# Gate, up, value and state-space gate projections as unit pairs with 512 moving weight columns

## What is computed

```python
def swiglu(u, w_gate, w_up, w_down):
    return (jax.nn.silu(u @ w_gate) * (u @ w_up)) @ w_down
...
    v = (mem_n @ wv).reshape(b, m, XATTN_HEADS, XATTN_HEAD_DIM)
...
    y = y.reshape(b, S, SSM_D_INNER) * jax.nn.silu(z.astype(jnp.float32))
```

## Time and profile before

| what | us |
|---|---|
| median of 3 runs | 2004.78 (2002.03 to 2006.02) |
| the profiled execution | 2001.61 |
| its span, first to last instruction | 1999.7 |
| TensorE busy | 1965.3 (98%) |
| GpSimd busy | 1567.7 (78%) |
| ScalarE busy | 1041.5 (52%) |
| VectorE busy | 720.5 (36%) |

### The profile page before, as it was taken

One profiled execution on the slowest core, in us unless ns is written; L12 is line 12 of the kernel. 1 busy time (PEld: TensorE's weight loads), 2 busy tenths in 40 slices (PEclk: granted clock), 3 DMA queues, 4 the chain that ended last, 5 costly groups with the idle time before them and its releaser, 6 DMA issues.

```text
span 1999.7 us, 34347 instructions
## 1 busy us (share of the span) xinstructions
PE 1965.3 (98%) x14430; PEld 1861.1 (93%) x14430; DVE 720.5 (36%) x1300; ACT 1041.5 (52%) x1342; POOL 1567.7 (78%) x1226
## 2 busy tenths in 40 slices
PE   7999999999999999999999999999999999999998
PEld 7999999988999999999999889999989999999997
DVE  2540866421200231037663320004687843022001
ACT  6434684456534554357644764346655556445333
POOL 7889786666888789878686759887686787789995
PEclk9999999999999999999999999999999999999999
DMA  8455543143555465554323445555433344445552
GB/s 319 170 199 189 186 144 114 64 169 134 203 190 189 173 231 182 187 181 178 127 78 135 169 150 188 190 190 196 147 127 120 127 156 148 158 179 195 181 185 104
DMA packets 48538, 332.60 MB, mean 166 GB/s; under 512 B 5376, under 2 KB 6272, under 8 KB 10112
## 3 DMA queue, kind: packets, MB, share of 16 engines
q1 hardware_dynamic: 43920, 314.60, 43.9%
q10 hardware_dynamic: 4464, 15.80, 2.3%
HBM read 329.33 MB, written 1.05 MB: 165 GB/s over the span
## 4 chain that ended last, share of the span: by engine, by line
PE 85%; DVE 6%; ACT 4%; POOL 1%; DVEq 1%; issue 1%; ACTq 1%; DMA 1%; SPq 0%
PE bank L1673 23%; PE bank L1674 23%; PE bank L1675 23%; ACT arena L371 2%; PE bank L1786 1%; POOL wlo L350 1%; PE bank L2029 1%; PE bank L2045 1%; ACT whi L371 1%; PE bank L1766 1%; PE bank L1768 1%; DVE x L1005 1%; DVE arena L978 1%; DVE bank L993 1%; PE bank L2152 1%
## 5 line engine op out<-in xcount | busy, mean ns | idle before, releaser
L350 POOL TENSOR_TENSOR wlo<-raw,whi 128x512 fp32r<-128x512 f32 x1188 | 1526.4, 1323 | 375.3 <-ACT whi L371 375.3
L1673 PE MATMUL bank<-uT_hi,whi 128*128 128x256 f32 x2560 | 731.5, 286 | 0.0
L1674 PE MATMUL bank<-uT_lo,whi 128*128 128x256 f32 x2560 | 725.2, 283 | 0.0
L1675 PE MATMUL bank<-uT_hi,wlo 128*128 128x256 f32 x2560 | 725.2, 283 | 0.0
L371 ACT ACTIVATE whi<-raw 128x2048 fp32r<-128x2048 f32 x297 | 566.8, 1910 | 170.0 <-PE bank L1675 152.3
L1673 PEld LDWEIGHTS bank<-uT_hi,whi 128*128 128x128 f32 x2560 | 491.6, 192 | 3.5 <-issue 1.4
L1674 PEld LDWEIGHTS bank<-uT_lo,whi 128*128 128x128 f32 x2560 | 491.6, 192 | 3.3 <-issue 1.4
L1675 PEld LDWEIGHTS bank<-uT_hi,wlo 128*128 128x128 f32 x2560 | 491.5, 192 | 0.0
L371 ACT ACTIVATE arena<-bank 128x512 f32<-128x512 f32 (+3 forms) x285 | 153.8, 554 | 337.6 <-PE bank L1675 264.9
L1053 DVE TENSOR_TENSOR bank<-arena,bank 128x512 f32<-128x512 f32 x50 | 34.8, 696 | 606.3 <-PE bank L1675 606.3
L1673 PE MATMUL bank<-whi,hT_hi 128*128 128x512 f32 x440 | 172.0, 391 | 0.0
(11 more groups left out here) (269 smaller groups left out, 2596.7 us busy)
## 6 DMA issues: line engine op xcount, KB each, us to landing
raw<-in_w SPq DMA_DIRECT2D x297, 1024.0 KB, 4.8
rows<-in_rows ACTq DMA_DIRECT2D x23, 512.0 KB, 4.9
arena<-in_mem ACTq DMA_DIRECT2D x2, 1024.0 KB, 7.2
x<-in_x SPq DMA_DIRECT2D x2, 512.0 KB, 6.4
out<-x SPq DMA_DIRECT2D x2, 512.0 KB, 2.7
arena<-in_amask ACTq DMA_DIRECT2D x1, 768.0 KB, 7.8
cst<-in_cst SPq DMA_DIRECT2D x1, 452.0 KB, 12.6
arena<-in_lvl SPq DMA_DIRECT2D x1, 384.0 KB, 13.9
```

Source lines behind the costliest of these rows:

```text
L350: r = pool.tensor_tensor(wlo[n % LAND][:, k], raw[n % LAND][:, k], whi[n % RING][:, k].bitcast(F32), ALU.subtract)
L1673: pe.matmul(o, l[0], r[0], start=start, stop=False)
L1674: pe.matmul(o, l[0], r[1], start=False, stop=False)
L1675: return pe.matmul(o, l[1], r[0], start=False, stop=stop)
```

## The change

- A new packing, `pair`, replaces two `cols` units by two units that each hold 512 columns over half of the depth (four 128-row blocks of 512 columns).
- `pair_unit` and `pair_half` work on them: for each half, token tile 0 into one bank and tile 1 into the other, 12 matmuls of 512 columns each. A new semaphore `tok_half` tells that tile 0 is complete, 12 matmuls before `unit_done` of the second unit.
- In a feed-forward block a bank now holds 256 gate columns and 256 up columns of one token tile. ACT and DVE work on each tile apart (256 columns an instruction), and the product goes to an SBUF buffer, `h_tok`. TensorE transposes it back in every chunk (`h_transposes`, two 128 x 128 transposes for each tile), after the down unit of the chunk before; in the last chunk one tile ahead of each half of the work of tile 0 in `last_rows`.
- `first_pair` runs on such pairs: for tile 0 high and low of half 0, high of half 1, the transposes of tile 1, low of half 1.
- Memory values (two pairs a layer), the first two retention value units, the first two units of the attention queries and the gates z use pairs as well. Their ACT readers wait for `tok_half` or for the second unit.

```diff
-                    act.wait_ge(sems["unit_done"], g + 1)
-                    fn(sg[q], bank[4 + 2 * q if c else 0][:, :], AF.Silu).then_inc(sems["silu_gate"], 1)
-                    split()
+                    if c:
+                        split()
                     if memory and c in (3, 4):
                         memory_hi(c - 3, (4, 6)[c - 3])
-                    if c:
-                        act.wait_ge(sems["ff_product"], p.count("ff_product"))
+                    for t in range(NT):
+                        if t == 0:
+                            act.wait_ge(sems["tok_half"], p.count("tok_half"))
+                        else:
+                            act.wait_ge(sems["unit_done"], u0 + (3 * c if c else 1) + 1)
+                        fn(sg[q][:, t * 256:(t + 1) * 256], bank[b[t]][:, 0:256], AF.Silu).then_inc(sems["silu_gate"], 1)
+                        if c == 0 and t == 0:
+                            split()
+                    if last:
+                        for t in range(NT):
+                            act.wait_ge(sems[f"act_bank{b[t]}"], p.count(f"act_bank{b[t]}"))
+                            fn(hT[0][:, 2 * q:2 * q + 2, t * P:(t + 1) * P],
+                               bank[b[t]][:, 0:256].rearrange("p (a b) -> p a b", a=2), AF.Copy).then_inc(sems["h_hi"], 1)
+                            if t == 0:
+                                root_table()
                     else:
+                        if c:
+                            split()
+                        act.wait_ge(sems[f"act_bank{b[0]}"], p.count(f"act_bank{b[0]}"))
+                        fn(hT[0][:, 2 * q:2 * q + 2, :], bank[b[0]][:, :].rearrange("p (a b) -> p a b", a=2), AF.Copy)\
+                            .then_inc(sems["h_hi"], 1)
+                    split()
...
+            def pair_half(w, b, src, t, half):
+
+                tk = slice(t * P, (t + 1) * P)
+                for k in range(4):
+                    c = slice(k * 512, (k + 1) * 512)
+                    r = mm3(bank[b][:, :], (src[0][:, 4 * half + k, tk], src[1][:, 4 * half + k, tk]), (w[0][:, c], w[1][:, c]),
+                            half == 0 and k == 0, half == 1 and k == 3)
+                return r
+
+            def pair_unit(banks, src, half, readers=None):
+
+                w = unit()
+                for t in range(NT):
+                    if half == 0 and readers:
+                        acquire(banks[t], readers)
+                    r = pair_half(w, banks[t], src, t, half)
+                    if half == 1 and t == 0:
+                        r.then_inc(sems["tok_half"], 1)
+                r.then_inc(sems["unit_done"], 1)
...
                 for c in range(1, CH):
...
+                    pair_unit(b, uT, 0)
+                    if c == 1:
+                        h_transposes(0, 0)
+                        h_transposes(0, 1)
...
+                    pair_unit(b, uT, 1)
                     if c < CH - 1:
                         h_ready()
...
                         proj_rows(hT, 2 - 2 * q, c == 1)
+                        h_transposes(c, 0)
+                        h_transposes(c, 1)
+
+                def second_tile():
+                    h_transposes(CH - 1, 1)
+                    h_ready()
                 q = (CH - 1) % 2
-                last_rows(hT, (2 - 2 * q, 2 * q), (h_ready, h_ready))
+                h_transposes(CH - 1, 0)
+                last_rows(hT, (2 - 2 * q, 2 * q), (h_ready, second_tile), h_ready)
...
+                    hi_phase(wa, a, 0, 0)
+                    lo_phase(wa, a, 0, 0)
                     wb = unit()
+                    hi_phase(wb, a, 0, 1)
+                    u_transposes(1)
+                    lo_phase(wb, a, 0, 1).then_inc(sems["tok_half"], 1)
...
+    def pair(m):
+
+        nonlocal n
+        w[n:n + 2] = m.reshape(2, 4, P, 512).transpose(0, 2, 1, 3).reshape(2, P, UNIT)
+        n += 2
```

More of the change, by code:

```diff
@@ L734, in _ @@
                 split_to(m0 + 28)
-                for h in range(2):
-                    act.wait_ge(sems["unit_done"], m0 + 28 + h + 1)
-                    fn(qtok[h], bank[h][:, :].rearrange("p (a b) -> p a b", a=2), AF.Copy).then_inc(sems["q_tok"], 1)
+                for t in range(NT):
+                    if t == 0:
+                        act.wait_ge(sems["tok_half"], p.count("tok_half"))
+                    else:
+                        act.wait_ge(sems["unit_done"], m0 + 30)
+                    fn(qtok_pair[:, :, t, :], bank[t][:, :].rearrange("p (a b) -> p a b", a=2), AF.Copy).then_inc(sems["q_tok"], 1)
                 split_to(m0 + 30)
@@ L1728, in proj_rows, with last_rows @@
                 r.then_inc(sems["unit_done"], 1)
-            def last_rows(src, k0, ready):
+            def last_rows(src, k0, ready, late=None):
                 w = [unit()]
@@ L1738, in last_rows @@
                                 w.append(unit())
+                        elif j and late:
+                            late()
                         for h in range(2):
@@ L1767, in hi_phase @@
+            def hi_phase(w, b, t, half, late=False):
+                pe.wait_ge(sems["u_hi"], p.count("u_hi"))
+                for k in range(4):
+                    c = slice(k * 512, (k + 1) * 512)
+                    u = uT[0][:, 4 * half + k, t * P:(t + 1) * P]
+                    pe.matmul(bank[b][:, :], u, w[0][:, c], start=half == 0 and k == 0, stop=False)
                     if not late:
-                        pe.matmul(o, u, w[1][:, c], start=False, stop=False)
-            def weights_lo_phase(w, b, t):
-                o = bank[b][:, t * SEQ:(t + 1) * SEQ]
+                        pe.matmul(bank[b][:, :], u, w[1][:, c], start=False, stop=False)
@@ L1773, in weights_lo_phase @@
+            def weights_lo_phase(w, b, t, half):
                 pe.wait_ge(sems["w_lo"], p.count("w_lo"))
[L1774 to L1787, removed]
+                for k in range(4):
+                    r = pe.matmul(bank[b][:, :], uT[0][:, 4 * half + k, t * P:(t + 1) * P], w[1][:, k * 512:(k + 1) * 512],
+                                  start=False, stop=half == 1 and k == 3)
+                return r
@@ L1788, in lo_phase @@
+            def lo_phase(w, b, t, half, late=False):
+                n = 4 + 2 * t + half
+                pe.wait_ge(sems[f"dve_read{n}"], p.count(f"dve_read{n}"))
+                del last_reader[n]
+                for k in range(4):
+                    r = pe.matmul(bank[b][:, :], uT[1][:, 4 * half + k, t * P:(t + 1) * P], w[0][:, k * 512:(k + 1) * 512],
+                                  start=False, stop=half == 1 and k == 3 and not late)
                 return r
@@ L2157, in query_T @@
                 def query_T():
+                    pe.wait_ge(sems["q_tok"], p.count("q_tok", 2))
+                    for h in range(2):
+                        del last_reader[h]
                     for h in range(2):
@@ L2210, in _ @@
                 if g:
[L2211 to L2212 removed]
+                    proj_pair(z_bank, "tok_out", uT)
                 pe.wait_ge(sems["conv_silu"], p.count("conv_silu"))
```

204 lines of the change are left out of this document (109 added, 95 removed).

## The result

| | us, median | runs |
|---|---|---|
| before, on the same chip | 2003.19 | 20 (2000.68 to 2006.03) |
| changed | 2009.07 | 20 (1999.24 to 2011.3) |

The ratio is 1.002 (1.0012 to 1.0029): the changed kernel is slower by 0.1 to 0.3%. Forecast were 1987.8 us and 1981 to 1997, so even the sign was wrong. The 20 runs lie on two levels: five at 1999.2 to 2000.6, fifteen at 2007 to 2011.3. Two executions of experiment 7 ran at a granted clock of 0.85 and 0.75 and are left out of its ratio.

The account below looks back on a forecast made before the run. TensorE's instruction stream, busy 98% of the span, was taken as the bound. Feed-forward blocks (8.9 and 2.5), first pairs 1.85, values 2.6 and z 1.2 gave 17.0 us off the 2004.78 median: 1987.8 us, range 1981 to 1997.

Parts of the forecast that it names:

- Do the transposes wait?: Feed-forward chunks: product ready at about 1.1 us, needed by the transposes at 5.46; cover 4.4 us, so cost nothing.
- keep their count and their order against `unit_done`: ACT's splits in feed-forward chunks: number and order unchanged; a wait for tile 0 stands behind one 1.9 us split only.
- The one that named this wait: No-change rival: GpSimd becomes the bound, or transposes wait for the product and eat 0.22 us per middle chunk; 5%.
- Slower: Rival: in pair units 512-column matmuls start 0.240 us apart, giving 2028 us, or 0.232, giving 2005.5; 5%.
- The pitch and the pair: Matmul units: 512-column matmuls start 0.2265 us apart; a whole pair falls from 11.52 to 10.87 us, gain taken as 0.64.
- the slow start: Nine down units inside a feed-forward block lose their slower first matmuls: 0.02 us each, 0.2 per block.
- The transposes: Chunks 1 to 10 get four new transposes each: 0.45 us per four, 4.05 us per feed-forward block.
- A middle chunk: Feed-forward chunk, from one down unit's start to the next: falls only from 16.98 to 16.76 us.
- The end of a block: Last feed-forward chunk: first square at 5.5 us instead of 4.8, four boundaries 0.7 us longer, the fifth block pays 0.45.
- The sum: Whole kernel: feed-forward blocks, other first pairs, values and z together gain 17.0 us, 0.85% faster.
- a first pair each: First pairs, ten of them: 0.37 us gained each; tile 0's 0.27 us turns into waiting.
- the gain of z: Three z pairs in layer 3: 1.9 us, less group 2's 0.64 lost to waiting and 0.1 for slack; 1.2 left.

Follow-up runs that it names:

- experiment 7: Changed kernel without a pause, memory scaling with one SBUF input, the multiplication with the row of weights left out: median 2006.88 us, ratio 0.9994.
- run 9: Changed kernel without a pause, ScalarE's second split put back behind the product's rounding in chunk 2 of two blocks: 1993.55 us, ratio 0.9955.
- run 6: run 1 with one transpose instead of two per token tile in chunks 1 to 9, part of the computation left out: 1985.72 us, ratio 0.9909.
- run 1: Changed kernel where GpSimd also waits for the memory scalings ahead of unit 8 of each of two layers: 1990.78 us, ratio 0.9933.
- run 4: run 1 with ACT's last split moved ahead of the rounding of tile 1 in a block's last chunk: 1989.50 us, ratio 0.9927.
- run 10: run 6 with GpSimd also waiting for the rotary angles ahead of unit 17, part of the computation left out: 1978.47 us, ratio 0.988.
- run 5: Changed kernel with GpSimd's pause for the memory scaling in layer 1 only: 1999.37 us, ratio 0.9974.
- run 8: The changed kernel executed once more, unaltered, for a second profile: 2009.4 us (one run).
- run 3: Kernel before the change with GpSimd's pause for the memory scalings in two layers: 2003.16 us, ratio 0.9997.
- run 2: Changed kernel without a pause, memory scaling moved on VectorE behind the two products of chunk 2: 2019.07 us, ratio 1.0076.

## Why the prediction was wrong

**The step that failed** is "Do the transposes wait? ... I cost it at nothing; cover is 4.4 us". The working took one undisturbed chunk and followed ScalarE's silu and VectorE's product through it. It never asked what else is queued on VectorE ahead of the product in the other 49 chunks. In two of them it is `memory_scale`, and there the product came 7.6 us late instead of 4.4 us early; with the lower clock behind each wait that is 21 us where nothing was put down. The row of 12.35 us for an instruction that takes 1.28 elsewhere was in the trace of before, and with it the figures for the loss: product at 64.34, and transposes due at about 63. That alone gives a wait of 2 to 3 us a layer, as run 9 measured (2.8); the further 4.8 us come from the split that the change moves ahead of the wait for the product. The forecast says of the splits only that they "keep their count and their order against `unit_done`"; their order against that wait changed.

**The rivals.** The one that named this wait had 5%, and wanted ScalarE late by 4.4 us "in every chunk". Late twice was enough, and it was VectorE that was late. The rival "Slower" got the sign right for a reason that did not happen, a pitch over 0.2296 us.

**The pitch and the pair** were nearly right. The distance between starts in a middle chunk is 0.2272 us on the mean (0.2265 forecast). In the dense part it is 0.2267, but the slow start is still there: behind the transposes the distances are 0.23 again for some six matmuls, as they were behind a change of width (from 574.72 to 576.11 below six take 1.39 us). The forecast took that slow start away.

**The transposes** cost 0.46 us for four (0.45 forecast), as this timeline of a middle chunk shows, beside the earlier trace rows; and run 6, which leaves out two of the four, is 0.24 a chunk shorter, so the price goes with the number.

```profile
573.58 0.60 PE L1933 MATMUL bank<-cst,arena 128*128 128x128 f32 x4
573.94 0.48 PE L1719 MATMUL bank<-whi,uT_hi 128*128 128x512 f32 x1
...
574.72 0.40 PE L1719 MATMUL bank<-whi,uT_hi 128*128 128x512 f32 x1
...
576.11 0.39 PE L1719 MATMUL bank<-whi,uT_hi 128*128 128x512 f32 x1
...
590.40 0.60 PE L1933 MATMUL bank<-cst,arena 128*128 128x128 f32 x4
```

A middle chunk takes 590.40 - 573.58 = 16.82 us, where 16.76 were forecast: 0.06 short, in 45 chunks 2.7 us.

**The end of a block** was right: last rows from 204.6, first square at 5.5 (ACT's timeline), to be read beside the earlier trace rows. The waits of the following u transposes grew by 0.2 to 0.4 us (0.3 forecast; 0.17 and 0.16 before, 0.35 and 0.52 in run 1, at the end of layer 1).

```profile
208.31 1.91 ACT L377 ACTIVATE whi<-raw 128x2048 fp32r<-128x2048 f32 x1
210.12 0.59 ACT L377 ACTIVATE arena<-bank 128x512 f32<-128x512 f32 x1
```

**The sum.** Without the stalls (run 1) 12.5 us are gained by the medians, and 10.7 by the profiled spans (1999.7 to 1989.0), where 17.0 were forecast. By stages of the two profiles, each counted from its own first `u_transposes` to those of the next stage:

| stage | gained, us | forecast |
|---|---|---|
| first feed-forward block, with the start-up | -0.2 | 2.2 |
| three feed-forward blocks with a boundary | 1.6 to 1.7 each | 2.2 each |
| last feed-forward block | 2.0 | 2.5 |
| two mixing stages, with the memory values | 3.4 together | 3.3 |
| two attention stages, a first pair each | 0.31 and 0.36 | 0.37 each |
| layer 3's branches, with z | -0.2 | 1.6 |

In each feed-forward block 0.5 us are the middle chunks, nine at 0.06. In layer 3's branches TensorE's listed waits grow from 8.6 to 10.6 us: the gain of z turned into waiting in more than group 2. In the first block TensorE waits 1.5 us for a split (`whi`) against 0.7 before, and in this profile the clock falls behind a wait of 2.3 us for `wlo`: it is 0.72 from 21 to 27 us, and 1.00 in the kernel before. Seven distances of 0.43 us and two somewhat longer ones cost about 1.6 us there. The profile of the changed kernel and those of runs 4, 7, 9 and 10 show the same fall in the start-up, those of runs 5, 6 and 8 do not, so it belongs to an execution and not to the change alone. With the pauses the median of 1989.5 to 1990.8 lies inside the range on record, without them it is 12 us above its end.

## What to carry to other kernels

Before a reader is moved closer to its writer, list everything that stands ahead of the writer on its engine, in every iteration and not in a typical one, and look for instructions whose duration differs between equal shapes: here a maximum ten times the minimum (12.35 against 1.28 us) was an instruction held by GpSimd, hidden only by slack that the change used up. Where GpSimd works without gaps, a short VectorE instruction on SBUF data can last until that run ends; a semaphore wait that makes a gap of 2.6 us ahead of a known victim cost nothing here (run 3) and was worth about 9 us for each stall avoided (runs 1 and 5). Moving the victim instead let the run go on longer (run 2). And a new wait costs more than its length: behind each 7.6 us of waiting stood another 2.8 at the lower clock.

## What the runs showed of the hardware

- A held VectorE instruction ended at a fixed time after GpSimd's unbroken run, whatever its own start: 1.08 or 1.09 us for the scalings, 0.15 or 0.16 for the casts (ends are start and duration added; layer 1):

| kernel | held from | GpSimd's run ends | it ends |
|---|---|---|---|
| before, scaling | 50.65 | 61.91 | 63.00 |
| changed | 52.32 | 67.97 | 69.05 |
| run 8 | 50.49 | 66.49 | 67.57 |
| run 1 | 52.32 | 53.08 | 54.17 |
| run 9 | 52.26 | 63.01 | 64.10 |
| run 2 | 57.32 | 76.60 | 77.68 |
| before, cast | 94.89 | 112.66 | 112.81 |
| run 6, cast | 97.73 | 109.43 | 109.59 |

- GpSimd isn't slowed by it: 24 subtractions in 29.96 us are 1.25 each, and 20 in 25.05 us in run 1, behind the pause, where no scaling was held, are 1.25 as well.
- TensorE's clock fell to 1.2 GHz after a wait of 2.8 us too (run 9: 0.51 from 66 to 69 us), and seven and five distances behind it were slow instead of twelve; after the start-up's wait of some 2 us it fell in some executions and not in others. How it depends on the wait stays open, and so does why a one-input instruction is held in some executions only (run 7), and why the changed kernel has two levels of time.
